# One token tile of a recurrence moved among the last gate products, an output product begun on its high weights, and small vectors loaded earlier

## The reference

```
u = rms_norm(h); z = u @ w_in + b_in
conv  = silu(layer_norm(conv31(a * sigmoid(gate)))) @ pw_w + pw_b        # a, gate: parts of z
h_t   = mLSTM(q, k, v, i, f)        # 4 heads, state of 256 x 128 per head, chunks
mlstm = (sigmoid(z_o) * rms_norm_per_head(h_t)) @ out_w
h = h + (sigmoid(z_gc) * conv + sigmoid(z_gm) * mlstm) @ w_out
h = h + top-4-of-32 mixture of SwiGLU experts(rms_norm(h))
out = rms_norm(h)[:, 16:]
```

## Time and profile before

| | |
|---|---|
| median of 3 runs | 1622.55 us (1622.53 to 1623.66) |
| the profiled execution's own time | 1622.37 us |
| its span in the trace | 1620.6 us |
| TensorE busy | 1581.8 us, 98% |
| VectorE, ScalarE, GpSimd busy | 649.2, 395.9, 425.9 us |
| mean granted TensorE clock | 0.992 |

### The profile page before, as it was taken

How to read it: one execution, slowest core, us unless ns; L and a number is a source line. 1 busy time by engine, 2 the same in 40 slices (tenths; PEclk the granted TensorE clock), 3 DMA queues, 4 the chain that set the end, 5 groups by cost and what they waited for, 6 DMA issues and landing times.

```text
span 1620.6 us, 38909 instructions
## 1 busy us (share of the span) xinstructions
PE 1581.8 (98%) x16458; PEld 921.9 (57%) x16458; DVE 649.2 (40%) x1244; ACT 395.9 (24%) x605; POOL 425.9 (26%) x465
## 2 busy tenths in 40 slices
PE   6999999998999899999999999999999999999997
PEld 6998988876889634443443344334443444444444
DVE  4799898016242624222422242223222322232247
ACT  5333134255221521111111111121112111211122
POOL 6334334372433621211121112111211121112114
PEclk9999999999999899999999999999999999999999
DMA  7553242320275289999999999999999999999995
GB/s 214 157 178 109 79 143 91 105 78 27 79 288 223 84 298 412 408 408 416 413 407 409 411 413 404 410 411 410 396 413 406 409 393 408 407 407 397 405 413 227
DMA packets 132292, 492.91 MB, mean 304 GB/s; under 512 B 17289, under 2 KB 74801, under 8 KB 82484
## 3 DMA queue, kind: packets, MB, share of 16 engines
q1 hardware_dynamic: 113876, 464.98, 72.9%
q0 software_dynamic: 8736, 16.22, 3.1%
q10 hardware_dynamic: 9632, 11.03, 2.1%
HBM read 476.32 MB, written 24.87 MB: 309 GB/s over the span
## 4 chain that ended last, share of the span: by engine, by line
PE 79%; DMA 11%; DVE 3%; ACT 2%; POOL 2%; SPq 2%; issue 1%; POOLq 0%; DVEq 0%; ACTq 0%
PE banks L1525 34%; PE banks L1097 25%; PE banks L1574 16%; DMA w_ring<-in_expert_w_dram 9%; PE banks L1512 1%; POOL slot_table L686 1%; DMA y_in<-y_rows 1%; DVE mix_lo L1887 1%; SPq L436 1%; PE banks L1612 1%; DMA small<-in_b_in_dram 0%; DMA y_rows<-y_out,row_now 0%; ACT banks L984 0%; ACT w_hi L793 0%; ACT conv L947 0%
## 5 line engine op out<-in xcount | busy, mean ns | idle before, releaser
L1525 PE MATMUL banks<-w_ring,xT 128*32 128x512 f32 x6144 | 671.3, 592 | 3.2 <-DMA w_ring<-in_expert_w_dram 2.4
L1525 PEld LDWEIGHTS banks<-w_ring,xT 128*32 128x32 f32 x6144 | 204.2, 110 | 429.8 <-issue 422.7
L1574 PE MATMUL banks<-w_ring,actT 128*32 128x256 f32 x6144 | 344.4, 380 | 0.0
L1574 PEld LDWEIGHTS banks<-w_ring,actT 128*32 128x32 f32 x6144 | 202.5, 110 | 137.5 <-issue 18.4
L2000 DVE TENSOR_TENSOR hid<-banks,bias 128x512 f32<-128x512 f32 x96 | 63.8, 665 | 474.4 <-PE banks L1525 474.4
L626 POOL TENSOR_TENSOR w_lo<-stage,w_hi 128x2048 fp32r<-128x2048 f32 x38 | 175.2, 4611 | 265.7 <-ACT w_hi L793 265.7
L1097 PE MATMUL banks<-u_hi,w_hi 128*128 128x264 f32 (+1 forms) x528 | 176.4, 334 | 0.3 <-ACT gates L907 0.3
L1097 PE MATMUL banks<-u_hi,w_lo 128*128 128x264 f32 (+1 forms) x528 | 175.2, 332 | 0.0
L1097 PE MATMUL banks<-u_lo,w_hi 128*128 128x264 f32 (+1 forms) x528 | 175.0, 331 | 0.0
L1058 ACT ACTIVATE bias<-banks 128x512 f32<-128x512 f32 x32 | 19.1, 597 | 560.4 <-PE banks L1545 560.4
L696 POOL COPY token_now<-token_of 96x1 int32 (+1 forms) x33 | 6.1, 184 | 565.9 <-PE banks L1512 561.3
(11 more groups left out here) (298 smaller groups left out, 1624.0 us busy)
## 6 DMA issues: line engine op xcount, KB each, us to landing
w_ring<-in_expert_w_dram SPq DMA_DIRECT2D x384, 1024.0 KB, 22.1
stage<-in_w_in_dram SPq DMA_DIRECT2D x20, 1024.0 KB, 5.1
stage<-in_w_in_dram SPq DMA_DIRECT2D x16, 512.0 KB, 5.2
y_rows<-empty_row ACTq DMA_DIRECT2D x8, 1024.0 KB, 4.7
y_in<-y_rows SPq DMA_DIRECT2D x4, 2048.0 KB, 21.9
stage<-in_conv_pw_w_dram SPq DMA_DIRECT2D x4, 1024.0 KB, 5.2
stage<-in_mlstm_out_w_dram SPq DMA_DIRECT2D x4, 1024.0 KB, 5.1
stage<-in_w_out_dram SPq DMA_DIRECT2D x4, 1024.0 KB, 5.3
```

The lines of the kernel that those rows point to most:

```text
L1525: last = nc.tensor.matmul(banks[32 * g:32 * (g + 1), t].rearrange("p (c j) -> p c j", j=64), xT[:, k, 32 * t:32 * (t + 1)], units, start=k ...
L1574: last = nc.tensor.matmul(banks[32 * g:32 * (g + 1), 3 + t, 0:GRP], actT[:, t, k], w2_ring[k // 2][:, k % 2, GRP * g:GRP * (g + 1)], start ...
```

## The change

It has three parts. In each, only the order and some waits change; the products are the same.

1. At the start, `load_glu` takes the slots to load. Slot 1 of pair 0 is loaded behind the twelve small transfers, ahead of `vb_bc`.
2. Tiles 20 to 23 are mixed with the recurrence of token tile 0. TensorE: tile 20 (bank 4), `state_part(0)`, tile 21 (bank 5), keys 1, tile 22 (bank 0), half of `state_part(1)`, numerators(0), tile 23 (bank 0) with the other half of `state_part(1)` and keys 2 inside it; then a wait for all sigmoids, and the tiles 1 to 3. ScalarE takes the matching order. The unused squares go to a buffer in SBUF, each waiting for the one before, and the numerators wait for VectorE's copy alone. `silu_rests(0)` on VectorE comes behind the state update of tile 0; GpSimd splits slot 1 of the `pw_w` pair behind the first tile's root.
3. In the first `w_out` pair, slot 1, the token tiles 0 and 1 are done in two passes: the two terms with `w_hi` after a wait for `w_hi` alone, then the term with `w_lo`.

```diff
-        mean_w, _ = take("mean_w", [P, P])
+        mean_w, mean_at = take("mean_w", [P, P])
+        head_squares = at("head_squares", [P, DV], F32, mean_at)
+        LAST_BANKS, LAST_TICKS = (4, 5, 0, 0), (1, 2, 5, 8)
...
-            def load_glu(n, first=False):
-                for s in range(2):
+            def load_glu(n, parts=range(2), first=False):
+                for s in parts:
...
-            load_glu(0, first=True)
+            load_glu(0, (0,), first=True)
...
+            load_glu(0, (1,), first=True)
             sp.dma_start(vb_bc, b_in[:, V_OFF:V_OFF + D].to_broadcast([P, D])).then_inc(row_bc_in, 16)
...
-            def split_pair(n):
-                for s in range(2):
+            def split_pair(n, parts=range(2)):
+                for s in parts:
...
-            split_pair(PW_PAIR)
+            split_pair(PW_PAIR, (0,))
...
                 nc.gpsimd.tensor_tensor(head_scale, head_rstd, den_inv, ALU.mult).then_inc(h_scaled, 1)
+                if i == 0:
+                    split_pair(PW_PAIR, (1,))
...
-            scaled_keys(0)
-            sigmoid_pair(5)
-            scaled_keys(1)
-
...
-            silu_highs(0)
-            for i in range(TT):
-
-                if i and i + 1 < TT:
-                    scaled_keys(i + 1)
+            def head_sums(i):
+
                 act.wait_ge(h_taken, i + 1)
                 for h in range(HEADS):
-                    nc.scalar.activation(banks[:, 4 + h, 0:DV], h_buf[i % 2][:, h], ACT.Square, scale=den_inv[:, h:h + 1],
+                    if i or h:
+                        act.wait_ge(h_squared, HEADS * i + h)
+                    nc.scalar.activation(head_squares, h_buf[i % 2][:, h], ACT.Square, scale=den_inv[:, h:h + 1],
                                          accum_out=head_square[:, h:h + 1]).then_inc(h_squared, 1)
+
+            def scaled_heads(i):
...
+            def last_sigmoid(t):
+
+                act.wait_ge(mm_done, pair_tick(SIG_PAIR + 5, LAST_TICKS[t]))
+                nc.scalar.activation(gates[:, 3 * KT - 4 + t], banks[:, LAST_BANKS[t]], ACT.Sigmoid,
+                                     bias=vec[:, B_SIG + 3 * KT - 4 + t:B_SIG + 3 * KT - 3 + t]).then_inc(sig_out, 1)
+
+            scaled_keys(0)
+            last_sigmoid(0)
+            last_sigmoid(1)
+            split_hi(PW_PAIR, 0)
+            scaled_keys(1)
+            last_sigmoid(2)
+            head_sums(0)
+            scaled_heads(0)
+            scaled_keys(2)
+            last_sigmoid(3)
+            split_hi(PW_PAIR, 1)
+            silu_highs(0)
+            for i in range(1, TT):
+                if i == 2:
+                    scaled_keys(3)
+                head_sums(i)
+                silu_highs(i)
+                scaled_heads(i)
+                split_hidden(i - 1)
...
-            sigmoid_tiles(5)
...
+            def numerators(i):
+
                 pe.wait_ge(head_out, HEADS + 1)
-                pe.wait_ge(h_squared, HEADS * i)
+                if i:
+
+                    pe.wait_ge(h_taken, i)
...
+                    if i == 2 and h == 2:
+                        key_transposes(3)
+
+            def last_sigmoid(t, within=None):
+                channel_tile(t // 2, t % 2, u, banks[:, LAST_BANKS[t]], main, 3 if t >= 2 else 1, within)
+
+            def rest_of_state():
+                state_part(1, (2, 3))
+                key_transposes(2)
+
+            wait_weights(SIG_PAIR + 5, 0)
+            pe.wait_ge(sig_out, 3 * KT - 5)
+            last_sigmoid(0)
+            state_part(0)
+            pe.wait_ge(sig_out, 3 * KT - 4)
+            last_sigmoid(1)
+            key_transposes(1)
+            wait_weights(SIG_PAIR + 5, 1)
+
+            pe.wait_ge(normed, KT)
+            last_sigmoid(2)
+            state_part(1, (0, 1))
+
+            pe.wait_ge(sig_out, 3 * KT - 2)
+            numerators(0)
+            pe.wait_ge(sig_out, 3 * KT - 1)
+            last_sigmoid(3, rest_of_state)
+            pe.wait_ge(sig_out, 3 * KT)
+            for i in range(1, TT):
+                numerators(i)
+                if i + 1 < TT:
                     hidden_transposes(i - 1, (0,))
...
-                    wait_weights(WO_PAIR + j, s)
+                    if j or s == 0:
+                        wait_weights(WO_PAIR + j, s)
...
-                    for i in range(TT):
+                    if j == 0:
+                        pe.wait_ge(w_hi_made[1], WO_PAIR + 1)
+                        for low in range(2):
+                            if low:
+                                wait_weights(WO_PAIR, 1)
+                            for i in range(2):
+                                span = slice(P * i, P * (i + 1))
+                                for k in range(KT):
+                                    terms = ((mix_hi, w_lo),) if low else ((mix_hi, w_hi), (mix_lo, w_hi))
...
+                    for i in range(0 if j else 2, TT):
...
             update_state(0)
-            silu_rests(0)
...
-                if i:
-                    silu_rests(i)
+                silu_rests(i)
```

More of the change, by code:

```diff
@@ L991, in _ @@
                                          scale=head_scale[:, h:h + 1]).then_inc(tok_made, 1)
-                if i:
-                    split_hidden(i - 1)
-                if i + 1 < TT:
-                    silu_highs(i + 1)
+            def last_sigmoid(t):
[21 more added lines that the diff above has]
+                split_hidden(i - 1)
             split_hidden(TT - 1)
@@ L1101, in weights, with channel_tile @@
                 return w_hi[:, s, k, P * c:P * (c + 1)], w_lo[:, s, k, P * c:P * (c + 1)]
-            def channel_tile(s, c, src, dst, span, ticks=None):
+            def channel_tile(s, c, src, dst, span, ticks=None, within=None):
                 hi, lo = src
                 for k in range(KT):
+                    if within and k == 5:
+                        within()
                     last = product(dst, weights(s, k, c), (hi[:, k, span], lo[:, k, span]), k)
@@ L1357, in hidden_transposes @@
                     last.then_inc(ht_mm, 1)
-            state_part(0)
-            pe.wait_ge(sig_out, 3 * KT)
-            for i in range(TT):
-                if i == 0:
-                    key_transposes(i + 1)
+            def numerators(i):
                 pe.wait_ge(head_out, HEADS + 1)
-                pe.wait_ge(h_squared, HEADS * i)
+                if i:
+                    pe.wait_ge(h_taken, i)
                 for h in range(HEADS):
@@ L1418, in _ @@
                         continue
-                    for i in range(TT):
+                    if j == 0:
[7 more added lines that the diff above has]
+                                    terms = ((mix_hi, w_lo),) if low else ((mix_hi, w_hi), (mix_lo, w_hi))
+                                    for m, (rows, w) in enumerate(terms):
+                                        last = nc.tensor.matmul(banks[:, 4 + i, GRP:2 * GRP], rows[:, k, span], w[:, 1, k],
+                                                                start=not low and k == 0 and m == 0, stop=low == 1 and k == KT - 1)
+                                if low:
+                                    last.then_inc(mm_done, 1)
+                    for i in range(0 if j else 2, TT):
                         token_tile(s, (mix_hi, mix_lo), banks[:, 4 * (1 - j) + i, GRP * s:GRP * (s + 1)],
```

## The result

The changed kernel takes 1625.24 us (median of 20 runs, 1621.45 to 1627.72) against 1623.13 us for the kernel before (20 runs, 1620.25 to 1625.12). The ratio is 1.0014, 95% interval 1.0008 to 1.0019: 2.3 us slower, clear of zero, and less than the 0.2% that I took as what a measurement can tell from none. The forecast was 1624.4 us, a change within that 0.2%.

What follows compares the result with a forecast made beforehand. TensorE, busy 98% of the time, was taken as the bound, with the chain ahead of the experts moving the end one to one. Recurrence +6.4, start -2.5, output projection -2.0: +1.9, 1624.4 us; eight in ten 1618.6 to 1628.5.

Steps and rivals of the forecast that it cites:

- Start: Before the first products: vectors' wait and low clock go (3.5 us), less 0.9 us waiting for slot 1; 2.5 us gained.
- Recurrence: Tiles 20 to 23 mixed with token tile 0: +3.4 us at full clock and +3.0 for clock drops, +6.4.
- (a): After tile 20, before the first state product: TensorE waits 3.2 us for ScalarE's scaled keys, kw_sb.
- (b): After tile 23, before numerators(1): TensorE waits 3.2 us for the late last sigmoid, until 373.4.
- (c): Before a state product after numerators(1): GpSimd's pass holds VectorE's silu subtractions, so TensorE waits 5.4 us.
- (d): Later in the recurrence: waits of 1.0, 0.9 and 1.4 us for scaled heads(1), scaled keys(3) and heads(2).
- Each drop costs half of 3.4, 1.7; I count a little under two: Recurrence: clock drops after long waits, a little under two of them falling into products, cost 3.0 us.
- signs of being wrong: No kw_sb wait, silu_lo at 0.68 us each, or more than one clock drop fewer or more than counted.
- Rival 2: Recurrence: GpSimd's pass does not hold VectorE's subtractions; wait 1.4 not 5.4 us, -4.0, 1620.4; with other luck 0.17.
- Output projection: First w_out pair: high products run while low weights are prepared, so TensorE's wait goes, -2.0 us.
- Rival 1: Start gives nothing, slot 1 landing at 28 or later: +4.4, 1627.0; 0.32 together with four clock drops in the recurrence.
- Rival 3: Recurrence: tiles 21 to 23 cover all waits and no new one appears, 1605 us; chance below 0.02.

Runs made afterwards that it cites:

- kernel 1: Kernel before with only the start's part (small vector loads ahead of slot 1 of the first weights): 1618.93 us, ratio 0.9981.
- kernel 4: Changed kernel with the 31 rows of convolution taps loaded in two transfers, of 16 and 15 rows: ratio to the kernel before 1.0012.
- kernel 2: Changed kernel with the start and output projection of before, so only the recurrence's part: 1631.23 us, ratio to the kernel before 1.0056.
- kernel 3: Kernel before with only the output projection's part of the change: 1622.52 us, ratio 0.9994.
- kernel 11: Kernel before with the start's and output projection's parts and the taps in two transfers, recurrence as it was: 1616.29 us, ratio 0.9958.
- kernel 6: Changed kernel with GpSimd's pass over slot 1 of the first pointwise weights one token tile later: 1621.28 us, ratio to the kernel before 0.9989.
- kernel 9: Changed kernel with VectorE's silu subtractions of tile 0 moved behind tile 1's state update and gating: 1621.50 us, ratio to the kernel before 0.9990.
- kernel 7: Changed kernel with the last sigmoid ahead of the scaled heads and scaled keys on ScalarE: 1626.42 us, ratio to the kernel before 1.0019.
- kernel 8: Changed kernel with taps in two, first state part behind tile 21, last sigmoid earlier, GpSimd's pass later: 1617.06 us, ratio to the kernel before 0.9966.
- kernel 10: Changed kernel with taps in two, state part later, sigmoid earlier and its wait behind numerators(1), tile 0's subtractions later: 1613.40 us, ratio to before 0.9937.

## Why the prediction came out, step by step

**Start, -2.5 predicted, -1.9 in the two traces, -3.1 in the times of kernel 1.** The vectors' wait and the low clock went, as said. The wait for slot 1 appeared, 1.3 us (0.9 predicted), its landing at 25.9 (25 to 25.5 predicted) behind the tap rows; kernel 4 shows that cause by taking it away. The term that was mis-sized is the low clock: I took the 3.4 us of the one trace, and it lasted 6.8 in the profiles of kernels 2 and 3.

**Recurrence, +6.4 predicted, +6.7 measured, and kernel 2 shows it alone (+6.6).** The places were right. (a) 3.2 predicted, 3.0 found. (b) 3.2 and 2.6. (c) 5.4 and 3.2. (d) 1.0 + 0.9 + 1.4; found 0.6 and 1.3. But the total is right by two errors that cancel. In this stretch TensorE's recorded waits are 10.9 us against 6.1; with the prediction's 0.25 us for each (six and seven waits), 12.4 against 7.9 (the prediction took 8.7), about +3.7 to +4.5, where I had +6.8. The remaining 2.2 to 3.0 of the 6.7 are put down to the clock, where I had 3.0 - 3.4 = -0.4.

The step that failed is "Each drop costs half of 3.4, 1.7; I count a little under two": three drops came, the one behind (a) lasted 6.8 us, and by the same estimate the 13.6 us of low clock, four times 3.4, cost some 6 us. More drops than counted was one of the signs of being wrong that the prediction named.

The two errors are linked: numerators(1) began 0.8 us later than I gave and took 5.3 us in place of 3.5 behind (b), at low clock, so that they ended at 379.6 in place of 376.9. Those 2.7 us came straight off (c), for which VectorE was ready at almost the time I gave (subtractions ended at 382.3, 381.6 predicted). The kernel before shows the same exchange: its clock was low ahead of the 2.20 us wait for the state update, and kernels 1, 3 and 11, where it was full there, waited 3.9 us at that place.

**The hold of (c), with VectorE until 381.6.** Kernels 6 and 9 show it by removing one side each. Kernel 7 shows that it came last: taking 2.5 us from (b) gives nothing. Rival 2 is settled with it; had the hold not been there, the recurrence would have been 3.9 us shorter (kernel 6). That its -4.0 fits is luck in part: it was worked out as a wait alone, and only 2.1 of the 3.9 are waits, the rest is the clock.

**Output projection, -2.0 predicted, -2.2 measured.** What I did not count is that the clock can fall behind that wait, as in kernel 2 (the window at 508.5, 1.5 us) but not in the profiles of the kernel before and of kernel 1.

**Sum.** -1.9 + 6.7 - 2.2 = +2.6 in the stretches, +2.3 by the ratio, +1.9 forecast. The range for eight in ten does not follow from its terms: rival 2 with the better start is 1619.4, not 1618.6, and rival 1 with one more drop 1627.0 + 1.7 = 1628.7, not 1628.5; nothing hangs on it here. Rival 1 (slot 1 at 27 or later) did not come: it was 25.9. Rival 3 was excluded by (a) and stays so: kernel 2 has all new waits.

What stays open: what sets the last 1085.4 to 1090.8 us from one execution to the next. The low clock in it does not put the profiles in order: it lasts 17.8 us in the kernel before (1086.6) and 8.8 in kernel 4 (1087.4). Open is also what makes a low stretch short or long behind the same wait.

## What to carry to other kernels

When work is moved to fill a wait, walk each engine's order again to find what was covering the next dependency: here one state part, moved by one gate tile, cost 5.5 us, more than the change lost. Move both sides of a conflict in thought: here a pass of 4.5 us on GpSimd was harmless beside VectorE work that reads PSUM and cost 3.9 to 4.3 us beside subtractions with both inputs in SBUF (kernels 6 and 8), and which of them it meets changes with every shift of the schedule (kernel 8). Remove the wait that comes last first; removing an earlier one alone (kernel 7) only lengthened the idle time, and the clock behind it.

## What the runs showed of the hardware

- The granted clock behind a wait is low for different times where the code ahead of it is the same: 3.4 us and 6.8 us behind the same wait of about 2 us, and 6.8 or 10.2 us behind (a). In the last part, which no kernel here alters, the low stretch 9 to 15 us behind the output projection lasts 3.4, 6.8 or 10.2 us by profile. With 7.5 us of idle it was low from 380.6 to 390.8, 5.8 us of it work (kernel 7).
- GpSimd is slowed as well: its root step took 1.33 us beside VectorE's subtractions (kernel 10) where it took 1.05 for tile 0 in the changed kernel, with VectorE idle.
- Behind a transfer of 31 rows all engines together moved 38 GB/s for two microseconds, while the weights were awaited; as 16 and 15 rows the same window has 282 GB/s.
